# Gate and up products with the tokens stationary and 512 weight columns moving, and h turned back by transposes

## What is computed

```
def rmsnorm(x, gain):
    y = x * rsqrt(mean(x * x, axis=-1, keepdims=True) + 1e-6)
    return y * gain

def swiglu(h, w_in, w_out):                 # w_in 1024 x 5632, w_out 2816 x 1024
    gate, up = split(h @ w_in, 2, axis=-1)
    return (silu(gate) * up) @ w_out

for l in range(2):                          # the first block
    x = x + 0.5 * swiglu(rmsnorm(x, ffn1_norm[l]), ffn1_w_in[l], ffn1_w_out[l])
    x = x + hybrid_mixer(rmsnorm(x, mix_norm[l]), ...)
    x = x + 0.5 * swiglu(rmsnorm(x, ffn2_norm[l]), ffn2_w_in[l], ffn2_w_out[l])
```

## Time and profile before

| | |
|---|---|
| median of 3 runs | 2391.69 us (2390.36 to 2392.84) |
| the profiled execution, first to last instruction (span) | 2391.4 us; no time of its own outside the span is shown |
| PE busy | 2351.3 us, 98% |
| PE weight loads busy | 2214.4 us, 93% |
| DVE busy | 1589.6 us, 66% |
| ACT busy | 1402.6 us, 59% |
| POOL busy | 145.8 us, 6% |
| memory read | 382.89 MB, 161 GB/s over the span |
| mean granted clock of PE | 0.997 of full |

### The profile page before, as it was taken

How to read it: one execution, slowest core, us unless ns; L and a number is a source line. 1 busy time by engine, 2 the same in 40 slices (tenths; PEclk the granted TensorE clock), 3 DMA queues, 4 the chain that set the end, 5 groups by cost and what they waited for, 6 DMA issues and landing times. The chain is left out here.

```text
span 2391.4 us, 40848 instructions
## 1 busy us (share of the span) xinstructions
PE 2351.3 (98%) x17170; PEld 2214.4 (93%) x17170; DVE 1589.6 (66%) x1952; ACT 1402.6 (59%) x1872; POOL 145.8 (6%) x119
## 2 busy tenths in 40 slices
PE   8999999999999999999999999999999999999998
PEld 7998999999999999899999999899999989999998
DVE  5666668856666756667875666659785455978554
ACT  5455778555555545678845655546754455675443
POOL 0000002200000000001400000000030000004000
PEclk9999999999999999999999999999999999999999
DMA  6555544235555556444415556544455654455653
GB/s 227 195 177 160 159 138 145 72 124 174 179 194 176 188 182 193 146 147 134 141 54 167 181 168 207 184 125 136 147 177 190 195 184 139 127 156 168 204 183 123
DMA packets 312453, 386.57 MB, mean 162 GB/s; under 512 B 10812, under 2 KB 287440, under 8 KB 312272
## 3 DMA queue, kind: packets, MB, share of 16 engines
q1 hardware_dynamic: 312160, 383.91, 49.8%
q10 hardware_dynamic: 112, 0.06, 0.0%
HBM read 382.89 MB, written 1.06 MB: 161 GB/s over the span
## 5 line engine op out<-in xcount | busy, mean ns | idle before, releaser
L313 PE MATMUL bank<-xhi,whi 128*128 128x256 f32 x3712 | 1064.8, 287 | 4.1 <-DVE wlo L302 4.1
L315 PE MATMUL bank<-xhi,wlo 128*128 128x256 f32 x3712 | 1052.3, 283 | 0.0
L314 PE MATMUL bank<-xlo,whi 128*128 128x256 f32 x3712 | 1052.2, 283 | 0.0
L292 DVE TENSOR_TENSOR wlo<-raw,whi 128x2048 fp32r<-128x2048 f32 x354 | 817.3, 2311 | 205.9 <-ACT whi L276 204.1
L276 ACT ACTIVATE whi<-raw 128x2048 fp32r<-128x2048 f32 x355 | 676.5, 1907 | 204.7 <-PE bank L315 204.7
L313 PEld LDWEIGHTS bank<-xhi,whi 128*128 128x128 f32 x3712 | 714.2, 192 | 9.3 <-DVE wlo L302 4.2
L314 PEld LDWEIGHTS bank<-xlo,whi 128*128 128x128 f32 x3712 | 714.3, 192 | 4.8 <-issue 1.9
L315 PEld LDWEIGHTS bank<-xhi,wlo 128*128 128x128 f32 x3712 | 713.7, 192 | 0.0
L313 PE MATMUL bank<-whi,yhi 128*128 128x512 f32 x608 | 237.9, 391 | 0.0
L314 PE MATMUL bank<-wlo,yhi 128*128 128x512 f32 x608 | 237.4, 390 | 0.0
L315 PE MATMUL bank<-whi,ylo 128*128 128x512 f32 x608 | 236.6, 389 | 0.0
(11 more groups left out here) (407 smaller groups left out, 2944.3 us busy)
## 6 DMA issues: line engine op xcount, KB each, us to landing
raw<-in_w_in SPq DMA_DIRECT2D x92, 1024.0 KB, 5.2
raw<-in_ffn_w_in SPq DMA_DIRECT2D x88, 1024.0 KB, 5.1
raw<-in_ffn_w_out SPq DMA_DIRECT2D x44, 1024.0 KB, 5.0
raw<-in_w_gate SPq DMA_DIRECT2D x32, 1024.0 KB, 5.6
raw<-in_w_up SPq DMA_DIRECT2D x32, 1024.0 KB, 5.4
raw<-in_w_down SPq DMA_DIRECT2D x32, 1024.0 KB, 4.9
raw<-in_w_branch_b SPq DMA_DIRECT2D x8, 1024.0 KB, 5.1
raw<-in_w_branch_a SPq DMA_DIRECT2D x8, 1024.0 KB, 5.4
```

Source lines behind the costliest of these rows:

```text
L292: e.tensor_tensor(wlo[s][:], raw[s][:], whi[s][:].bitcast(F32), ALU.subtract).then_inc(lo_done[s], 1)
L313: e.matmul(o, ahi, bhi, start=start, stop=False, skip_group_check=True)
L314: e.matmul(o, ahi, blo, start=False, stop=False, skip_group_check=True)
L315: return e.matmul(o, alo, bhi, start=False, stop=stop, skip_group_check=True)
```

## The change

Gate and up are computed the other way round. The tokens are stationary (128 tokens of xhi or xlo) and the weights move, 512 columns at a time: 256 gate columns and the 256 up columns of the same features side by side. A unit holds these 512 columns for one half of the 1024 input features ("A" the first half, "B" the second), so that a block is A, B and the down unit D, and the same 1 MB each. A unit of kind A or B is loaded by two DMAs of 512 KB, and counts twice on the semaphore. The result has tokens on partitions, bank t for token half t, gate in its left half and up in its right half. So 1/rms is a scalar per partition: ACT applies it to the gate as it copies it out of PSUM (two activations of 256 columns in place of DVE's scale_gate), DVE applies it to up in gate_h, and the spread product goes away in these stages. h now has tokens on partitions, and PE turns it back by four 128 by 128 transposes (turn_h) into the bank whose gate and up have been read. hhi and hlo are made from that bank. The turn of block i stands between the two token halves of B of block i+1, and the down product of block i-2 follows B of block i. hhi and hlo have four buffers in place of two. The tail turns the last h after the first part of the last but one down unit. The second block's stages keep the spread.

```diff
-U_FFN1 = 3 * FF1_BLOCKS
+FFN1_ORDER = [(w, i) for i in range(2) for w in "AB"]
+for block in range(2, FF1_BLOCKS):
+    FFN1_ORDER += [("A", block), ("B", block), ("D", block - 2)]
+FFN1_ORDER += [("D", FF1_BLOCKS - 2), ("D", FF1_BLOCKS - 1)]
+FFN1_AT = {what: at for at, what in enumerate(FFN1_ORDER)}
+U_FFN1 = len(FFN1_ORDER)
...
-        def last_rows(e, n1, a1, n2, a2, ready2, j):
+        def last_rows(e, n1, a1, n2, a2, ready2, j, after_first=None):
             split_ready(e, n1)
             if j in LATE_AT:
                 row_part(e, n1, *a1, 0, 0)
+                if after_first is not None:
+                    after_first()
                 row_part(e, n1, *a1, 1, 0)
                 row_part(e, n1, *a1, 0, 1)
...
-        def up_bank(i):
-            return bank[5 + i % 2 * 2]
...
+        def gate_up_bank(i, t):
+            return bank[4 + i % 2 * 2 + t]
+        def as_half(w):
+            return w[:, 0:UNIT].rearrange("p (c n) -> p c n", c=4)
...
+            def half_of(i, k, h):
+                return w_in[l, k * 512:(k + 1) * 512, h * FF1 + i * 256:h * FF1 + (i + 1) * 256].rearrange("(c p) n -> p c n", p=P)
...
+                if kind == "D":
+                    load_unit(e, unit(r0, u0 + at), rows_of(i), as_out)
+                else:
+                    s, _ = n = unit(r0, u0 + at)
+                    load_unit(e, n, half_of(i, "AB".index(kind), 0), of_gate)
+                    e.dma_start(as_half(raw[s])[:, :, 256:512], half_of(i, "AB".index(kind), 1)).then_inc(raw_in[s], 16)
...
-            def gate_up(i):
-                if i >= 2:
-                    e.wait_ge(h_done, f * FF1_BLOCKS + i - 1)
-                if i:
-                    feature_product(e, gate_unit(r0, u0, i), gate_of(i), xhi, xlo)
-                else:
-                    late_first_product(e, gate_unit(r0, u0, i), gate_of(i), j, first)
-                    spread_pe(e, j)
-                feature_product(e, up_of(r0, u0, i), up_bank(i), xhi, xlo)
+            def half_product(i, k, between=None):
+                kind = "AB"[k]
+                n = ffn1_unit(r0, u0, kind, i)
+                s, _ = n
+                late_start = i == 0
+                def part(t, chunks):
+                    for c in chunks:
+                        if late_start and t == 0:
+                            chunk_ready(e, j, 4 * k + c)
+                        mm = product3(e, gate_up_bank(i, t)[:], xhi[:, 4 * k + c, t * P:(t + 1) * P],
+                                      xlo[:, 4 * k + c, t * P:(t + 1) * P], as_half(whi[s])[:, c, :], as_half(wlo[s])[:, c, :],
+                                      k == 0 and c == 0, k == 1 and c == 3)
+                    return mm
...
+                split_ready(e, n)
+                part(0, range(4))
+                if between is not None:
+                    between()
+                part(1, range(4)).then_inc(multiplied[s], 1)
+            def turn_h(i):
+                e.wait_ge(h_done, f * FF1_BLOCKS + i + 1)
+                o = gate_up_bank(i, 0)
+                for c in range(2):
+                    for t in range(TT):
+                        mm = e.transpose(o[:, c * T + t * P:c * T + (t + 1) * P],
+                                         hbuf[:, t * T + c * P:t * T + (c + 1) * P], ident)
+                mm.then_inc(h_turned, 1)
             def h_ready(i):
                 e.wait_ge(hhi_done, f * FF1_BLOCKS + i + 1)
                 e.wait_ge(hlo_done, 1 + f * FF1_BLOCKS + i + 1)
-            gate_up(0)
+            half_product(0, 0, lambda: turn_half(e, j, 1, 1))
+            half_product(0, 1)
             for i in range(1, FF1_BLOCKS):
-                gate_up(i)
-                if first and i == FF1_BLOCKS - 1:
-                    e.wait_ge(h_done, i)
-                    setup_pe(e)
-                h_ready(i - 1)
-                if i == 1:
-                    e.wait_ge(spread_done, late(j) + 1)
-                if i < FF1_BLOCKS - 1:
-                    row_product(e, unit(r0, u0 + 3 * i + 1), hhi[(i - 1) % 2], hlo[(i - 1) % 2], i == 1)
+                if i >= 2:
+                    e.wait_ge(hlo_done, 1 + f * FF1_BLOCKS + i - 1)
+                half_product(i, 0)
+                half_product(i, 1, lambda: turn_h(i - 1))
+                if i >= 2:
+                    h_ready(i - 2)
+                    row_product(e, ffn1_unit(r0, u0, "D", i - 2), hhi[(i - 2) % 4], hlo[(i - 2) % 4], i == 2)
             i = FF1_BLOCKS - 1
-            last_rows(e, unit(r0, u0 + 31), (hhi[(i - 1) % 2], hlo[(i - 1) % 2]),
-                      unit(r0, u0 + 32), (hhi[i % 2], hlo[i % 2]), lambda: h_ready(i), j + 1)
+            if first:
+                setup_pe(e)
+            h_ready(i - 1)
+            last_rows(e, ffn1_unit(r0, u0, "D", i - 1), (hhi[(i - 1) % 4], hlo[(i - 1) % 4]),
+                      ffn1_unit(r0, u0, "D", i), (hhi[i % 4], hlo[i % 4]), lambda: h_ready(i), j + 1, lambda: turn_h(i))
...
             def exp_of_gate(i):
                 n = f * FF1_BLOCKS + i
-                e.wait_ge(gate_dve, n * 3 + SCALED)
+                s, r = ffn1_unit(r0, u0, "B", i)
+                e.wait_ge(multiplied[s], r + 1)
                 e.wait_ge(gated, 1 + n)
+                if i == 0:
+                    e.wait_ge(late_norm, late(j) * 5 + SCALE_READY)
+                for t in range(TT):
+                    up = e.activation(gbuf[:, t * T:(t + 1) * T], gate_up_bank(i, t)[:, 0:T], ACT.Copy, scale=rstd[:, t:t + 1])
+                up.then_inc(gate_act, 1)
+                e.wait_ge(gate_act, n * 5 + SCALED)
                 e.activation(eg, gbuf, ACT.Abs).then_inc(gate_act, 1)
...
                 e.activation(eg, eg, ACT.Exp, scale=-1.0).then_inc(gate_act, 1)
...
                 e.activation(eg, eg, ACT.Ln, bias=one).then_inc(gate_act, 1)
             def sigmoid_of_gate(i):
                 n = f * FF1_BLOCKS + i
-                e.wait_ge(gate_dve, n * 3 + LOG_SIGMOID)
+                e.wait_ge(gate_dve, n + 1)
                 e.activation(eg, eg, ACT.Exp).then_inc(gate_act, 1)
             def split_h(i):
-                e.wait_ge(h_done, 1 + f * FF1_BLOCKS + i)
-                if i >= 2:
-                    s, r = unit(r0, u0 + 3 * i - 2)
+                e.wait_ge(h_turned, f * FF1_BLOCKS + i + 1)
+                if i >= 4:
+                    s, r = ffn1_unit(r0, u0, "D", i - 4)
                     e.wait_ge(multiplied[s], r + 1)
-                e.activation(hhi[i % 2].rearrange("p c t -> p (c t)"), hbuf, ACT.Copy).then_inc(hhi_done, 1)
-            split_hi(e, unit(r0, u0 + 2))
-            spread_act(e, j)
+                e.activation(hhi[i % 4].rearrange("p c t -> p (c t)"), gate_up_bank(i, 0)[:], ACT.Copy).then_inc(hhi_done, 1)
+            def split_at(at):
+                split_hi(e, unit(r0, u0 + at))
+            split_at(2)
+            split_at(3)
             for i in range(FF1_BLOCKS):
-                if first and i == FF1_BLOCKS - 1:
+                exp_of_gate(i)
+                first_split, *other_splits = splits_after(i)
+                split_at(first_split)
+                sigmoid_of_gate(i)
+                for at in other_splits:
+                    split_at(at)
+                split_h(i)
+                if first and i == FF1_BLOCKS - 3:
                     setup_act(e)
-                if i:
-                    split_hi(e, unit(r0, u0 + 3 * i + 1))
-                exp_of_gate(i)
-                split_hi(e, unit(r0, u0 + (3 * i + 2 if i else 3)))
-                sigmoid_of_gate(i)
-                if 0 < i < FF1_BLOCKS - 1:
-                    split_hi(e, unit(r0, u0 + 3 * i + 3))
-                split_h(i)
+        def splits_after(i):
+            last = FFN1_AT["B", i + 1] + 2 if i + 1 < FF1_BLOCKS else U_FFN1 - 1
+            return range(FFN1_AT["B", i] + 3, last + 1)
...
-            def scale_gate(i):
-                n = f * FF1_BLOCKS + i
-                s, r = gate_unit(r0, u0, i)
-                e.wait_ge(multiplied[s], r + 1)
-                if i == 0:
-                    e.wait_ge(spread_done, late(j) + 1)
-                e.tensor_tensor(two(gbuf), two(gate_of(i)[:]), spread_two(), ALU.mult).then_inc(gate_dve, 1)
-                e.wait_ge(gate_dve, n * 3 + SCALED)
-                e.tensor_tensor(two(gbuf2), two(gbuf), spread_two(), ALU.mult).then_inc(gate_dve, 1)
             def log_sigmoid_of_gate(i):
                 n = f * FF1_BLOCKS + i
...
                 e.scalar_tensor_tensor(eg, gbuf, 0.0, eg, ALU.min, ALU.subtract).then_inc(gate_dve, 1)
             def gate_h(i):
                 n = f * FF1_BLOCKS + i
-                s, r = up_of(r0, u0, i)
-                e.wait_ge(gate_act, n * 4 + SIGMOID)
-                e.wait_ge(hlo_done, 1 + n)
-                e.wait_ge(gate_dve, n * 3 + SCALED_TWICE)
-                e.tensor_tensor(hbuf, eg, gbuf2, ALU.mult).then_inc(gated, 1)
+                e.wait_ge(gate_act, n * 5 + SIGMOID)
```

(83 more changed lines are left out.)

59 lines of the change are left out of this document (26 added, 33 removed).

## The result

The changed kernel takes 2398.59 us (median of 6 runs, 2397.68 to 2401.61) against 2391.32 for the kernel before in the same session (6 runs, 2390.36 to 2392.84): a ratio of 1.0030 with a 95% interval of 1.0018 to 1.0041. It is slower by 0.3%. The forecast was 2396.8, slower by 0.2%, in a range of 2386 to 2404: direction, size and range hold. The profiled execution has a span of 2399.0 us, 7.6 more than before; its own time is 2400.8, so 1.8 us lie outside the span.

A forecast was written before the change was run, and what follows sets the result against it. PE, busy 98% of the span, was taken to set the pace alone. Its stream -10.8, waits +13.9 and clock +2.0 gave +5.1 us on a span of 2391.4, 0.3 below the runs' median: 2396.8 us, range 2386 to 2404.

The forecast's parts named there:

- The block: PE's stream per feed-forward block: 16.78 us instead of 16.98, so -8.8 us over 44 blocks.
- Rival 4: Products moving weights beside stationary tokens save nothing when wide: 0.65 us more a block, 2425; shares 0.17 with other slower cases.
- The chain of h: From B of a block issued (T) through ACT and DVE: h done at T + 8.70, PE starts at T + 8.80.
- The waits: PE waiting at turns of blocks 0, 1 and last, and at stage starts: 5.1 + 7.4 + 1.4 = +13.9 us, bounds 11 to 17.
- the last turn: Last block's turn of h: PE waits 2.0 us in three stages and 1.4 in the first.
- B: B of block 0, at a stage's start, waits for the late split of x: 0.45 us in three stages, +1.4.
- The clock: Half clock for 3.4 us behind some new long PE waits, 1.7 us each: +2 us, between 0 and 6.8.
- The sum: -10.8 + 13.9 + 2.0 = +5.1 us on a span of 2391.4, giving 2396.8 us.
- - 1.7: The spread product dropped from the four stages: 0.43 us each, -1.7 us in all.
- - 0.3: PE's brief wait for hlo at a stage's end goes in three stages: 0.1 us each, -0.3 us.
- Rival 1: Faster: h is early and PE hardly waits at the turns, all waits under 6 us; all hidden, 2380.6; chance 0.10.

The follow-up runs named there:

- narrow products: Changed kernel with each 512-column product of gate and up issued as two of 256: 2421.25 us, 1.0118 of the kernel before.
- single transpose: Changed kernel with only one of the four transposes of h made in each block: 2384.68 us, 0.9969 of the kernel before.
- first three experiments: Changed kernel with the weight split moved behind silu's last step and the multiplications: block 10 2389.82 us, blocks 0 and 1 2397.99, all three 2387.42.
- early start: Changed kernel with silu's last step and the multiplications ahead of the weight split in blocks 0 and 1 alone: 2397.99 us, 1.0019 of before.
- early-x: Changed kernel with the transposes of x's last quarter after 6, not 12, matmuls of a stage's first unit: 2400.19 us, 1.0032 of before.

## Why the prediction was right

- **The block:** 16.78 forecast, 16.80 measured. The saving is 0.18 and not 0.20, since 512 columns take 227 and not 226.5 ns; over 44 blocks -7.9 instead of -8.8. The narrow products and the single transpose show both parts of it apart: +0.6 for what the width saves, -0.33 for three transposes.
- **Rival 4** fell: a matmul of 512 moving weight columns takes 227 ns and not twice the 120 of 256 columns. The Trainium skill's gap formula ("TensorE: Matmul & The Clock Gate", Back-to-back issue gap), which that section gives for isolated matmuls, 109 and 216 ns, would have made the block longer than 16.98. The traces of this case do not agree with it: the block became shorter.
- **The chain of h:** T is 599.78, where A of block 1 starts. DVE's logarithm step starts at 602.94, its low half at 604.75, gate at 606.96 and up at 607.68, in this timeline:

```profile
602.94 0.69 DVE L859 SCALAR_TENSOR_TENSOR arena<-arena 128x512 f32<-128x512 f32 x1 [3.72 <-ACT arena L778]
604.75 2.29 DVE L312 TENSOR_TENSOR wlo<-raw,whi 128x2048 fp32r<-128x2048 f32 x1 [1.12 <-ACT whi L296]
606.96 0.69 DVE L864 TENSOR_TENSOR arena<-arena 128x512 f32<-128x512 f32 x1
607.68 0.88 DVE L868 SCALAR_TENSOR_TENSOR arena<-bank,rstd,arena 128x256 f32<-128x256 f32 x2
```

  These are T + 4.97, 7.18 and 7.90 for the last three (forecast 4.96, 7.17 and 7.88), h done at T + 8.78 (8.70) and PE at T + 8.83 (8.80). PE was there at 607.94, T + 8.16 as forecast. A chain of seven steps on three engines came out within 0.1 us, because each step was taken from a row of the same instructions in the same neighbourhood. That the weight split in its middle is what makes it late, the first three experiments show.
- **The waits:** 14.2 against 13.9; 2.03 against 2.0 for the last turn, 1.28 against 1.4 in the first stage, 0.46 against 0.45 for B.
- **The clock:** +2.0 forecast. The one execution shows the stretch at 767.6; each costs 1.6. In six profiled executions whose last turns wait (this one, the second of the same kernel, the early start, narrow, single-transpose and early-x kernels), 6 of 18 such waits of 2.0 us were followed by one. That gives 3 x 1/3 x 1.6 = 1.6 us a run. In the three kernels whose last turns in those stages do not wait, none of 9 was followed by one. A test that keeps the wait but keeps PE busy was not made, so the waits as the cause of these stretches are seen, not shown.
- **The sum:** forecast +5.1 on the span, measured +7.6. -7.9 - 1.7 - 0.3 + 14.2 = +4.3; the other 3.3 are clock or not attributed: one stretch behind the last turn and one in the first mixer that no changed instruction explains, less one that the rest of the program lost.
- **What was mis-sized:** the median moved by 7.3 us (2391.32 to 2398.59), and 5.1 were forecast. Of the missing 2.2, 0.9 is the block's saving (7.9 for 8.8) and 0.3 the waits; the other 1.0 is clock or not attributed. The median came out only 1.8 above the 2396.8 since the six runs of the kernel before have a median 0.4 below that of the three from which the forecast started.
- **Time and span:** the forecast says that the span is 0.3 below the median of the runs. That 0.3 compares the profiled execution with other ones. A run's time is 1.8 us above its own span (2400.8 and 2399.0), so the profiled execution of the kernel before took about 2393.2 us, an estimate by that difference, longer than any of the six runs beside it. It does not harm the forecast, which comes to adding 5.1 to a median.
- **Rival 1** had named its condition: only a list without the weight split in the middle would hide the waits, for 2380.6 us. With that list the kernel measures 2382.5, on a chip whose runs of before are 1.3 us above the recorded median.

## What to carry to other kernels

When PE is at 98% and a change moves a product's operand through another engine, count two things: PE's stream per block, and at every place where PE's list is shorter than in the middle of the loop (first blocks, last block) the time from the last input to the result against the work PE still has. Here a gain of 10 us in the stream became a loss of 7 because the same order of ACT's and DVE's lists was kept for three blocks of eleven that have no slack; moving a weight split behind the urgent result in those three, with two small edits at the start, turned it into a gain of 10. And look at what was hidden behind the wait that you remove: a late load stood there.

## What the runs showed of the hardware

- A half-clock stretch does not always cost time. Where PE sets the pace it costs 1.6 us (above). In the mixer behind the fourth stage the changed kernel's second execution has one at 1618.8, ahead of a wait for DVE, and the wait shrinks by as much. The waits at line 2158 in the first and in the second execution of the changed kernel:

```profile
1637.54 0.55 PE L2158 MATMUL bank<-table,arena 128*128 128x128 f32 x3 [1.82 <-DVE arena L2390]
```

```profile
1635.89 0.55 PE L2158 MATMUL bank<-table,arena 128*128 128x128 f32 x3 [0.21 <-DVE arena L2390]
```

  So the mean granted clock of a run tells little of its time: the second execution has a mean of 0.994 as the first has, and its span is 3.2 us shorter. From the last turn of the fourth stage to this product both executions take 108.4 us, with the stretch and without it. All kernels of this study scatter by 2 to 4.5 us from run to run, which is why differences of 1 to 2 us were left open here.
- Transposes of 128 by 128 (float32) between products cost PE 0.11 us each when three are taken out, and 0.44 for four with the slow first product behind them: in these rows from 66.00 to 66.35, and 0.09 more in the next interval.

```profile
65.77 0.39 PE L335 MATMUL bank<-whi,xlo 128*128 128x512 f32 x1
66.00 0.60 PE L712 MATMUL bank<-table,arena 128*128 128x128 f32 x4
66.35 0.48 PE L333 MATMUL bank<-whi,xhi 128*128 128x512 f32 x1
66.67 0.40 PE L334 MATMUL bank<-wlo,xhi 128*128 128x512 f32 x1
```
